# Twenty rows instead of 128 in ten small matmuls, and no memset for the rows that were padding

## The reference

```python
def rms_norm(x, g):
    xf = x.astype(jnp.float32)
    y = xf * lax.rsqrt(jnp.mean(xf * xf, axis=-1, keepdims=True) + EPS)
    return (y * g.astype(jnp.float32)).astype(x.dtype)
...
    q_x, k_x, v_x = jnp.split(h_x @ w_qkv, [qd, qd + kvd], axis=-1)
    q_x = rope_2d(rms_norm(q_x.reshape(B, S, N_HEADS, HEAD_DIM), q_gain), tables)
    k_x = rope_2d(rms_norm(k_x.reshape(B, S, N_KV_HEADS, HEAD_DIM), k_gain), tables)
    k_c = rms_norm(k_c.reshape(B, L, N_KV_HEADS, HEAD_DIM), k_gain)
```

## Time and profile before

| | before |
|---|---|
| median of 3 runs | 2621.58 us (2619.35 to 2622.94) |
| profiled execution, own time | 2619.35 us |
| its span, first to last instruction | 2617.5 us |
| PE busy | 2497.2 us, 95% |
| DVE busy | 1525.9 us, 58% |
| ACT busy | 1264.8 us, 48% |
| mean granted TensorE clock | 0.985 |
| chain that ended last | PE 84%, DVE 7%, DMA 3%, ACT 3% |

### The profile page before, as it was taken

The page is one execution under the profiler, slowest core; times in us unless marked ns, Lnnn a source line. Parts: engine busy times, 40 slices in busy tenths (PEclk is TensorE's granted clock), DMA queues, the critical chain, the costliest instruction groups (busy, mean ns, idle before and its releaser), DMA issues.

```text
span 2617.5 us, 42439 instructions
## 1 busy us (share of the span) xinstructions
PE 2497.2 (95%) x15422; PEld 2131.7 (81%) x15422; DVE 1525.9 (58%) x2430; ACT 1264.8 (48%) x1950; POOL 133.6 (5%) x108
## 2 busy tenths in 40 slices
PE   5989899999989998999999999999999999999998
PEld 3845578888878985788888999898888899989887
DVE  2445544332254246666677666777767766576874
ACT  1436623222233343455555458655555545864553
POOL 3000000000000000000000002110000000211000
PEclk8999999999999999999999999999999999999999
DMA  8258623332223341465565555356656555544653
GB/s 263 73 161 267 220 86 97 96 96 94 92 81 113 104 153 49 145 186 176 185 192 169 177 170 171 119 156 191 183 183 184 161 186 170 160 145 145 186 183 120
DMA packets 398653, 398.25 MB, mean 152 GB/s; under 512 B 17360, under 2 KB 396768, under 8 KB 398544
## 3 DMA queue, kind: packets, MB, share of 16 engines
q1 hardware_dynamic: 395680, 390.25, 48.1%
q0 software_dynamic: 2864, 6.57, 0.8%
HBM read 395.72 MB, written 1.05 MB: 152 GB/s over the span
## 4 chain that ended last, share of the span: by engine, by line
PE 84%; DVE 7%; DMA 3%; ACT 3%; issue 2%; SPq 0%; POOL 0%; DVEq 0%; ACTq 0%
PE acc L814 32%; PE acc L808 24%; PE acc L810 12%; PE acc L793 4%; DMA raw<-in_ada_w_dram 3%; DVE w_lo L1730 3%; ACT w_hi L1188 1%; PE acc L870 1%; PE wk L937 1%; PE acc L839 1%; PE wk L889 1%; PE wk L964 1%; PE acc L1157 1%; PE wk L879 1%; PE acc L964 1%
## 5 line engine op out<-in xcount | busy, mean ns | idle before, releaser
L1730 DVE TENSOR_TENSOR w_lo<-raw,w_hi 128x1024 fp32r<-128x1024 f32 (+1 forms) x656 | 815.5, 1257 | 625.2 <-ACT w_hi L1188 623.6
L1188 ACT CAST w_hi<-raw 128x1024 fp32r<-128x1024 f32 (+1 forms) x656 | 669.3, 1032 | 462.9 <-PE acc L814 229.8
L814 PE MATMUL acc<-h_all,w_hi 128*128 128x256 f32 (+1 forms) x3360 | 748.9, 319 | 20.7 <-DVE w_lo L1730 6.6
L808 PE MATMUL acc<-h_all,w_hi 128*128 128x512 f32 x2016 | 713.0, 399 | 4.5 <-DVE h_all L1839 4.5
L814 PEld LDWEIGHTS acc<-h_all,w_hi 128*128 128x128 f32 x3360 | 562.1, 192 | 65.7 <-issue 14.9
L810 PE MATMUL acc<-h_all,w_lo 128*128 128x256 f32 x2016 | 564.9, 280 | 0.0
L814 PE MATMUL acc<-h_all,w_lo 128*128 128x256 f32 (+1 forms) x1680 | 534.5, 318 | 0.0
L808 PEld LDWEIGHTS acc<-h_all,w_hi 128*128 128x128 f32 x2016 | 380.1, 189 | 97.4 <-issue 4.7
L810 PEld LDWEIGHTS acc<-h_all,w_lo 128*128 128x128 f32 x2016 | 381.7, 189 | 0.2
L814 PEld LDWEIGHTS acc<-h_all,w_lo 128*128 128x128 f32 x1680 | 323.1, 192 | 20.6
L808 PE MATMUL acc<-hid_all,w_hi 128*128 128x512 f32 x880 | 311.6, 397 | 3.0 <-DVE w_lo L1730 3.0
(11 more groups left out here) (343 smaller groups left out, 2485.4 us busy)
## 6 DMA issues: line engine op xcount, KB each, us to landing
raw<-in_w_in_dram SPq DMA_DIRECT2D x100, 512.0 KB, 3.9
raw<-in_ada_w_dram SPq DMA_DIRECT2D x96, 512.0 KB, 5.2
raw<-in_ffn_w_in_dram SPq DMA_DIRECT2D x88, 512.0 KB, 3.6
raw<-in_ffn_w_gate_dram SPq DMA_DIRECT2D x88, 512.0 KB, 3.9
raw<-in_ffn_w_up_dram SPq DMA_DIRECT2D x88, 512.0 KB, 4.0
raw<-in_ffn_w_down_dram SPq DMA_DIRECT2D x80, 512.0 KB, 4.3
raw<-in_ret_w_qkvg_dram SPq DMA_DIRECT2D x48, 512.0 KB, 3.7
raw<-in_ffn_w_out_dram SPq DMA_DIRECT2D x40, 512.0 KB, 3.5
```

Source lines behind the costliest of these rows:

```text
L808: pe.matmul(o, w_hi[:, s, k, c], merged[:, :, kk, t], start=(u == 0 and k == 0), stop=False, skip_group_check=True)
L814: mm = pe.matmul(o, ws[:, s, k, c], xs[:, kk, t], start=(u == 0 and k == 0 and i == 0), stop=(last and k == nk - 1 and i == 2))
L1188: act.copy(w_hi[:, s, 0:nk, :], raw[:, s, 0:nk, :]).then_inc(hi_done, 1)
L1730: dve.tensor_tensor(w_lo[:, s, 0:nk, :], raw[:, s, 0:nk, :], w_hi[:, s, 0:nk, :], ALU.subtract).then_inc(lo_done, 1)
```

## The change

Three things go. DVE no longer clears `sd_b`, ACT no longer waits for that, and the ten matmuls L1026 take only the partitions 0 to 19 of both operands. Columns, outputs and everything around them are as before.

```diff
-        sd_zero = sem("sd_zero")
...
-                    pe.matmul(wk[:, 1 + c % 2, :], headback[:, HEAD_ORDER[c], :], sd_b[:, 0, :], start=True, stop=True).then_inc(hback, 1)
+                    pe.matmul(wk[:, 1 + c % 2, :], headback[0:20, HEAD_ORDER[c], :], sd_b[0:20, 0, :], start=True, stop=True).then_inc(hback, 1)
...
             act.wait_ge(hss, 10)
-            act.wait_ge(sd_zero, 1)
             act.activation(sd_b[0:20, 0, :], wk[0:20, 0, :], ACT.Sqrt, bias=eps[0:20, 0:1], scale=1.0 / HD).then_inc(hstd, 1)
...
-            dve.memset(sd_b[:, 0, :], 0.0).then_inc(sd_zero, 1)
             dve.wait_ge(in_attn, 96)
             dve.wait_ge(hstd, 1)
             dve.reciprocal(sd_b[0:20, 0, :], sd_b[0:20, 0, :]).then_inc(hrec, 1)
```

## The result

The changed kernel takes 2637.53 us (four runs, 2636.25 to 2638.82) against 2621.16 us before (2619.35 to 2622.94): 0.62% slower, ratio 1.0062 with an interval of 1.0045 to 1.0080. The profiled execution of the changed kernel took 2634.45 us; it isn't among the four and is faster than all of them. Forecast were 2623.6 us and no measurable difference, in a range that ended at 2627.5. The forecast was wrong. The rival "slower, by the clock", with 2639.3 us and a chance of 0.05, is what happened: TensorE stayed at the lower of its two clock levels through the whole stage.

A forecast was written before the change was run, and what follows sets the result against it. PE was taken to bound the stage, in rounds of 2.06 us. Terms 0, 0, 0, +2.2 and -0.2 gave +2.0 us on the median 2621.58: 2623.6 us, range 2618.0 to 2627.5.

The forecast's parts named there:

- slower, by the clock: Rival: 20-row matmuls keep TensorE's clock at its lower level to the stage's end; about 2639 us, chance 0.05.
- Memset and wait: DVE's removed 0.48 us memset and ACT's wait for it are covered by DVE idling of 29.19 us: 0.
- Streaming: The ten L1026 matmuls on 20 rows stream their 512 columns as long as before: 0, at best 0.1 us less.
- Changes of shape: Around the 20-row L1026: 9 new ways out of a narrow shape and 2 in, +2.2 us, range 0 to 2.6.
- What becomes of it: After the stage's delay, loads that PE waits for may land sooner: 0.2 of the 2.2 us given back.
- the sum: Whole kernel: memset 0, wait 0, streaming 0, shape changes +2.2, given back -0.2, together +2.0 us.
- two rows: Evidence against a lasting low clock: 1.00 during head sums on 20 of 128 columns, and from 200 to 240 us.
- it decides once the lower level lasts 6.4 us longer than now: Threshold for a lasting low clock: 3.2 us of work take twice as long, with the 2.0 making 5.2 us, 0.2%.
- The faster rival: L1026's weights load while L870 still streams, saving 1.2 us over six steady rounds; 2620.3 us, chance 0.07.
- over half: Argument for a lasting low clock: L1026 makes up over half of a round's streaming time.
- the three changes counted at the lower level: Three new shape changes placed between 151.60 and 155.20, at 1.2 GHz, costing 3 by 0.19 us more at most.

The follow-up runs named there:

- rows20_memset: Kernel before with only the ten L1026 matmuls cut to 20 rows, memset and ACT's wait kept; ratio 1.0078 (1.0050 to 1.0105).
- fill_after: Changed kernel plus four extra 128-row matmuls of 512 columns on PE during DVE's reciprocal; ratio 1.0061 (1.0037 to 1.0084) to the kernel before.
- fill_before: Kernel before plus four extra 128-row matmuls of 512 columns on PE during DVE's reciprocal; ratio 1.0003 (0.9989 to 1.0017).
- rows64_pair: Kernel before with L1026 on 64 rows, each with a companion matmul on rows 64 to 127 into an unread bank; ratio 1.0010 (0.9993 to 1.0027).
- rows64: Kernel before with the ten L1026 matmuls on 64 rows, without companions; ratio 1.0051 (1.0024 to 1.0078).
- the version with halves: Against the kernel before: factors split onto partitions 0-63 and 64-127, paired 256-column matmuls, no memset; 2612.07 us against 2619.91, ratio 0.9973.

## Why the prediction was wrong, point by point

- **Memset and wait: 0.** Right. DVE's idling and ACT's releaser are as before, and rows20_memset and the changed kernel lose alike.
- **Streaming: 0.** Right at a given clock: two matmuls of 20 rows take 1.98 us in fill_after, two of 128 rows 1.98 in fill_before. In the changed kernel one took 2.00 us where it had taken 1.06 because the clock was at its lower level.
- **Changes of shape: +2.2.** The mechanism was right, and so was the size at the full clock: L1032 behind a narrow matmul takes 0.63 against 0.43 (rows64_pair), 0.20 where I took 0.18. At the low clock it is 1.15 against 0.85, so 0.30; 9 ways out and 2 ways in come to 3.3 us in the changed kernel. The rule of the Trainium skill that a change of tiling mode drains TensorE ("TensorEngine Tiling (Array Packing)", "Tiling Modes") fits both, in that every change has a price; whether it is the drain or the load that is paid, these runs can't tell. rows64_pair, with the forecast's changes of shape and the clock back at 157, has a ratio of 1.0010 (0.9993 to 1.0027), which leaves room for this term and little more.
- **What becomes of it: all but 0.2 is kept.** Held: of 19.0 us at the start of attention 18.7 are left at its end.
- **The failed step: the sum has no term for the clock.** It lets the lower level end at about 155.2 as before, and leaves what the 20-row matmuls do to the clock to a rival with a chance of 0.05. Measured: the lower level lasted to about 191, and the stage took 18.4 us more in place of 2.2. The rival had the mechanism and the place, and nearly the price: it puts the end of the stage at 170.86, where the chain leaves PE, but one L1032 and four L870 follow until 172.0. With them its 15.7 + 2.0 becomes 16.8 + 2.0, against the 18.4.
- **Why that chance was so low.** I set it on two rows, and both were misread. The head sums at a clock of 1.00 use 20 output columns but all 128 rows; they say nothing on rows. The stretch from 200 to 240 at 1.00 with the 64-row L937 in it has its matmuls in pairs on both halves of the array, which I had noted myself under the shapes and didn't carry over. Put as rows64 and rows64_pair, it is the case with the companion, not without it. No row of before showed a matmul that left half of the rows idle for more than a moment, so nothing there spoke against the rival, and its chance should have been near the forecast's.
- **The clock's return.** The statement "it decides once the lower level lasts 6.4 us longer than now" fits: 80 rows, with some 8 us longer and no changes of shape to pay, lose 0.17%; 64 and 20 rows, with some 35, lose 0.5 to 0.8%.
- **The faster rival.** Wrong: the load in front of L1026 stays in the open (rows64_pair: 0.62 for the first pass against 0.42 for the second).
- **Two small misreadings that change nothing.** L1026 streams for 0.86 us of a round of 2.06, which is over half only with the load in front of it. And of the three changes counted at the lower level the last, at 155.75, lies behind the clock's return.

## What to carry to other kernels

Zero rows in a matmul aren't waste to be trimmed: here they cost no time, and with them TensorE's clock was at 2.4 GHz for everything around them. Before cutting the contraction of matmuls that make up much of PE's time in a stretch, look in the profile for a stretch with as few rows at work at once, and read its granted clock; if there is none, price the stretch at the lower level with a real chance. Where the rows are to be used better, put a second piece of the work on them, side by side, as the version with halves does.

## What the runs showed of the hardware

- Under matmuls on 20 rows the granted clock went from 1.00 to 0.50 although PE had idled for only 0.6 us, and stayed there for 35 us and more (fill_after, 154 to 189). PE's busy share in the profile doesn't tell this: it read 100%. The Trainium skill ("TensorE: Matmul & The Clock Gate", "Part 1: The HAM clock gate") has the gate released by how busy PE is; in these runs being busy wasn't enough.
- Rows that multiply zeros by zeros keep the clock up like others (96 and 128 rows, and the companion of rows64_pair, whose operands are all zero). On output columns there is one place only: the head sums, with 20 of 128 columns, ran for 3.8 us at a clock of 1.00.
- A weight load in the open costs 0.20 us at 2.4 GHz and 0.30 at 1.2 GHz, both into a narrow shape (L1026 behind L870) and out of one (L1032 behind L1026). Behind 80 and 96 rows L1032 has none.
